# The projection of the last attention head spread over two heads, in a fused block of pooling, stick-breaking attention, delta net and MLP

## The chip, the cores and the metric

The kernel runs on one core of a Trainium2 chip, as one launch. The metric is the device time of that launch in microseconds (us). Times inside the program are counted from the start of the span of the profiled execution. The engines are TensorE (PE), VectorE (DVE), ScalarE (ACT), GpSimd (POOL) and the queue of SyncE (SP) that issues the DMAs.

## What is computed

Input x has 1024 tokens of 1024 channels, float32. Four blocks follow one another: a pooling mixer, a stick-breaking attention mixer, a gated delta net, a squared-ReLU MLP, with RMS norms between. Only the second matters here. With u the normed stream (1024 x 1024):

```
proj = u @ w_in                       # 1024 -> q 1024, k 1024, v 2048, z 2048
q, k: 16 heads of 64;  v: 16 heads of 128
z_ts = q_t . k_s / 8
A[t,s] = sigmoid(z_ts) * prod_{s<j<t} (1 - sigmoid(z_tj)),  s < t
o = A @ v
y = o * silu(z)
h = h + y @ w_out
```

## The kernel before, in words

**Numbers.** Each float32 operand of a large product is kept as a rounded part (hi) and the rest (lo), and a product is three matmuls: hi*hi, lo*hi, hi*lo. ACT rounds and DVE subtracts. For weights these are `split_weights` in both engines (L1078 and L1415), on tiles of 128 x 1024.

**The projection of a head** is three weight tiles: q and k together (64 + 64 columns), v, and the gate. Each is multiplied with all 1024 tokens in two halves of 512, each half in 8 chunks k of the contraction. `gemm_part(tile, h, k0, k1, rhs)` (L750) issues chunks k0 to k1 of half h, three matmuls for each chunk (L761 to L763), into PSUM bank 0 or 1 in turn. A projection is thus 6 halves of 8 chunks. One chunk of one half is called a unit here: 48 units, numbered in this order, 0 to 15 for q and k, 16 to 31 for v, 32 to 47 for the gate.

**A head of the attention** is NS = 12 steps. `step_of(n)` gives the piece: steps 0 to 3 and 4 to 7 are the triangular blocks of the two key halves (width 128, 256, 384, 512), steps 8 to 11 the full 512 x 512 block. Every step goes through the engines in a fixed chain:
- TensorE: `logits(n)` (L782, L783), two matmuls into banks 2 to 4
- ACT: `take_logits(n)`, sigmoid of both signs into `beta` and `stick_left`
- POOL: `mask(n)` (L536, L537) in the triangular steps
- DVE: `scan(n)` (L1523), the running product
- POOL: `weigh(n)` (L543), beta times the product, and a start value for the next scan (L548 or L553)
- TensorE: `turn_weights(n)` (L791), transposes into banks 5 and 6
- ACT: `round_weights(n)` (L1158); DVE: `rest_of_weights(n)` (L1530)
- TensorE: `values` (L804 to L806), the product with v into bank 7, once for each of three groups of four steps

**The order of work is written out by hand.** Each engine runs its own function `slots(b, first, end, ...)`, which in slot n issues the logits of step n + 3, the scan of n + 2, and the turning, rounding and rest of step n; b is the buffer of the head (0 or 1). Engines take their instructions strictly in this order and wait on semaphores. In the same slots stands the projection of the next head: TensorE issues four units a step (two ahead of and two behind `turn_weights`), DVE evacuates and scales them (`stage` into `staged` and `v_staged`, L1539; `take_gate`, L1559), `split_qk(1 - b)` splits q and k (ACT L1161 to L1163, DVE L1544 to L1548), `turn_v` (L772) transposes v through bank 7 and `split_v` (ACT L1166, DVE L1553) takes it. The gate takes its sigmoid on ACT in step 1 of its own head (L1169), two products on POOL in steps 2 and 3 (L560), and is multiplied with the output by DVE's `take_o` (L1568): half 0 in step 6, half 1 in step 1 of the next head. SP stores the output of the head to DRAM (L333).

**Loop and tail.** A loop of seven turns runs heads 0 to 13, two a turn, each with slots 2 to 11 of head b and slots 0 and 1 of the next. Written out behind it stand `slots(0, 2, NS)`, head 14 with the projection of head 15 (40 units in steps 2 to 11; units 0 to 7 are done in steps 0 and 1, in the loop), and `slots(1, 0, NS, project=False, last=True)`, the last head, without a projection. In the last head SP loads the mixed outputs of heads 0 to 7 back (`mixed_early`, L366 and L370), and ACT (L1192) and DVE (L1597) split them into the state buffers in steps 6, 7, 8, 10 and 11, as `EARLY` says. The output projection (L702 to L704) follows.

What the change touches are the four `slots` functions (POOL, TensorE, ACT, DVE), the calls of them behind the loop, and one argument in `values`.

## Time and profile before

| | us |
|---|---|
| median of 3 runs | 3315.76 |
| lowest, highest | 3312.76, 3315.87 |
| profiled execution | 3315.06 |
| its span | 3313.0 |
| TensorE busy | 3177.2 (96%) |
| DVE busy | 1723.6 (52%) |
| ACT busy | 1047.9 (32%) |
| POOL busy | 533.9 (16%) |

The span is what the profile covers, and the profiled execution's own time is 2.06 us longer. Busy time of TensorE counts overlapping matmuls once; a matmul of 512 columns is shown as lasting 0.40 us while the next one starts 0.23 us after it, so starts are to be compared, not durations. The granted clock (PEclk) is a share of full speed: 1.00 is 2.4 GHz and 0.50 is 1.2 GHz. In a row of a timeline "x4" means that four instructions are drawn together, and a bracket says how long the engine was idle before and what released it. Head 14 and the last head lie between about 1426 and 1512 us.

### The profile page before, as it was taken

The page shows a single profiled execution, that of the slowest core. Times are in us where ns is not written, and L with a number is a line of the kernel's source. Part 1 is how long each engine was busy: PE and PEld are TensorE (multiplying, and loading weights), DVE is VectorE, ACT ScalarE, POOL GpSimd, SP SyncE. Part 2 cuts the span into 40 slices and gives each one's busy share as a digit, 9 for nine tenths or more (in the row PEclk, how much of TensorE's full clock was granted, in tenths as well). Part 3 has the DMA queues.
Part 4 walks back from the last instruction along what each step waited for, and adds up shares of the span by engine and source line. Part 5 has one row for each costly group of instructions (what it writes and reads, how often), then busy time and mean ns, then how long its engine had stood idle before and what let it go on. Part 6 is the DMA issues. An engine that isn't in the chain of part 4 may idle for free.

```text
span 3313.0 us, 41664 instructions
## 1 busy us (share of the span) xinstructions
PE 3177.2 (96%) x14874; PEld 2561.5 (77%) x14874; DVE 1723.6 (52%) x1984; ACT 1047.9 (32%) x1364; POOL 533.9 (16%) x1003
## 2 busy tenths in 40 slices
PE   6999999999999999998995999999979999999998
PEld 4888888868888888877854788888767788888886
DVE  4555555647767767774233555555534423333343
ACT  3212111145545545542142444444422211111112
POOL 0000000004434434440001222222202000000001
PEclk9999999999999999999997999999969999999999
DMA  3111111121111111114103111111121111111111
GB/s 87 48 45 50 44 51 44 51 76 39 45 34 48 51 35 41 51 64 159 56 14 92 36 35 35 35 35 35 36 64 45 45 48 48 44 45 50 45 51 64
DMA packets 287554, 167.30 MB, mean 50 GB/s; under 512 B 79352, under 2 KB 273912, under 8 KB 287232
## 3 DMA queue, kind: packets, MB, share of 16 engines
q1 hardware_dynamic: 287488, 166.41, 17.3%
q8 instruction: 43, 0.70, 0.1%
q14 instruction: 23, 0.19, 0.0%
HBM read 144.33 MB, written 22.05 MB: 50 GB/s over the span
## 4 chain that ended last, share of the span: by engine, by line
PE 91%; DVE 4%; issue 1%; ACT 1%; SPq 1%; POOL 0%; DMA 0%; DVEq 0%; ACTq 0%; POOLq 0%
PE banks L702 16%; PE banks L704 16%; PE banks L703 16%; PE banks L761 8%; PE banks L762 8%; PE banks L763 8%; PE banks L791 2%; PE banks L953 1%; PE banks L894 1%; PE banks L946 1%; PE banks L711 1%; PE banks L804 1%; PE banks L806 1%; PE banks L805 1%; PE banks L783 1%
## 5 line engine op out<-in xcount | busy, mean ns | idle before, releaser
L761 PE MATMUL banks<-state_a_hi,weights_hi 128*128 128x512 f32 x1296 | 554.5, 428 | 20.9 <-DVE conv_in L1695 13.5
L762 PE MATMUL banks<-state_a_lo,weights_hi 128*128 128x512 f32 x1296 | 513.7, 396 | 0.0
L763 PE MATMUL banks<-state_a_hi,weights_lo 128*128 128x512 f32 x1296 | 513.4, 396 | 0.0
L702 PE MATMUL banks<-state_a_hi,weights_hi 128*128 128x512 f32 x1280 | 509.0, 398 | 1.9 <-DVE state_a_lo L1759 1.9
L704 PE MATMUL banks<-state_a_hi,weights_lo 128*128 128x512 f32 x1280 | 507.1, 396 | 0.0
L703 PE MATMUL banks<-state_a_lo,weights_hi 128*128 128x512 f32 x1280 | 507.0, 396 | 0.0
L1078 ACT ACTIVATE weights_hi<-weights_raw 128x1024 fp32r<-128x1024 f32 x225 | 236.7, 1052 | 646.6 <-PE banks L704 635.7
L1415 DVE TENSOR_TENSOR weights_lo<-weights_raw,weights_hi 128x1024 fp32r<-128x1024 f32 x225 | 301.1, 1338 | 137.4 <-ACT weights_hi L1078 135.1
L761 PEld LDWEIGHTS banks<-state_a_hi,weights_hi 128*128 128x128 f32 x1296 | 246.8, 190 | 62.7 <-DVE weights_lo L1415 13.9
L763 PEld LDWEIGHTS banks<-state_a_hi,weights_lo 128*128 128x128 f32 x1296 | 244.9, 189 | 58.4
L702 PEld LDWEIGHTS banks<-state_a_hi,weights_hi 128*128 128x128 f32 x1280 | 241.1, 188 | 61.0 <-DVE state_a_lo L1759 2.3
L703 PEld LDWEIGHTS banks<-state_a_lo,weights_hi 128*128 128x128 f32 x1280 | 241.1, 188 | 58.8 <-issue 0.8
L704 PEld LDWEIGHTS banks<-state_a_hi,weights_lo 128*128 128x128 f32 x1280 | 240.9, 188 | 58.3
L762 PEld LDWEIGHTS banks<-state_a_lo,weights_hi 128*128 128x128 f32 x1296 | 247.0, 191 | 37.5 <-issue 1.9
L1523 DVE TENSOR_TENSOR_SCAN stick_left<-stick_left,eps_column 128x128 f32<-128x128 f32 (+1 forms) x192 | 241.6, 1259 | 39.1 <-POOL beta L537 33.2
L702 PE MATMUL banks<-state_b_hi,weights_hi 128*128 128x512 f32 x640 | 253.5, 396 | 0.0
L704 PE MATMUL banks<-state_b_hi,weights_lo 128*128 128x512 f32 x640 | 253.1, 396 | 0.0
L703 PE MATMUL banks<-state_b_lo,weights_hi 128*128 128x512 f32 x640 | 253.1, 395 | 0.0
L543 POOL TENSOR_TENSOR beta<-beta,stick_left 128x128 f32<-128x128 f32 (+1 forms) x192 | 167.5, 872 | 424.3 <-DVE stick_left L1523 424.3
L1874 DVE TENSOR_TENSOR stream_again<-stream_again,banks 128x512 f32<-128x512 f32 (+1 forms) x80 | 54.8, 685 | 267.2 <-PE banks L704 267.2
L1530 DVE TENSOR_TENSOR weights_T_lo<-banks,weights_T_hi 128x128 fp32r<-128x128 f32 (+1 forms) x192 | 103.8, 541 | 126.7 <-ACT weights_T_hi L1158 126.7
L1158 ACT ACTIVATE weights_T_hi<-banks 128x128 fp32r<-128x128 f32 (+1 forms) x192 | 94.7, 493 | 236.7 <-PE banks L791 236.7
(265 smaller groups left out, 4788.0 us busy)
## 6 DMA issues: line engine op xcount, KB each, us to landing
weights_raw<-in_mlp_w_dram SPq DMA_DIRECT2D x64, 512.0 KB, 3.6
weights_raw<-in_gdn_w_in_dram SPq DMA_DIRECT2D x33, 512.0 KB, 4.0
weights_raw<-in_pool_w_in_dram SPq DMA_DIRECT2D x32, 512.0 KB, 3.8
weights_raw<-in_sb_w_in_dram SPq DMA_DIRECT2D x32, 512.0 KB, 4.0
weights_raw<-in_pool_w_out_dram SPq DMA_DIRECT2D x16, 512.0 KB, 3.5
weights_raw<-in_sb_w_in_dram SPq DMA_DIRECT2D x32, 256.0 KB, 4.6
mixed_dram<-stick_gate SPq DMA_DIRECT2D x16, 512.0 KB, 3.3
weights_raw<-in_sb_w_out_dram SPq DMA_DIRECT2D x16, 512.0 KB, 4.9
```

What stands on the lines that cost most here:

```text
L543: ins = pool.tensor_tensor(b, b, left[c][:, HALF - w + 1:HALF + 1], ALU.mult)
L702: pe.matmul(psum[:, bank, :], whi, hi, start=(k == 0), stop=False)
L703: pe.matmul(psum[:, bank, :], whi, lo, start=False, stop=False)
L704: last = pe.matmul(psum[:, bank, :], wlo, hi, start=False, stop=(k == kc - 1))
L761: pe.matmul(psum[:, bank, :], whi, hi, start=(k == 0), stop=False)
L762: pe.matmul(psum[:, bank, :], whi, lo, start=False, stop=False)
L763: last = pe.matmul(psum[:, bank, :], wlo, hi, start=False, stop=(k == KC - 1))
L1078: act.activation(w_hi[slot][:, :], raw[slot][:, :], ACT.Copy).then_inc(weights_hi, 1)
L1158: act.activation(aT_hi[r][:, 0:w // P, c * P:c * P + P], psum[:, 5 + n % 2, 0:w].rearrange("p (j q) -> p j q", q=P), ACT.Copy).then_inc(a_ ...
L1415: dve.tensor_tensor(w_lo[slot][:, :], raw[slot][:, :], w_hi[slot][:, :].bitcast(F32), ALU.subtract).then_inc(weights_lo, 1)
L1523: dve.tensor_tensor_scan(v, v, eps_col[:, 2:3].to_broadcast([P, w]), left[c][:, HALF:HALF + 1], ALU.mult, ALU.add).then_inc(stick_scanned, 1)
L1530: dve.tensor_tensor(aT_lo[r][:, 0:w // P, c * P:c * P + P], psum[:, 5 + n % 2, 0:w].rearrange("p (j q) -> p j q", q=P), hi, ALU.subtract). ...
```

## The change

The 40 units that steps 2 to 11 of head 14 held are spread over 16 steps, from step 2 of head 14 to step 5 of the last head: step s (counted on into the last head as 12 to 17) issues units 8 + 40(s-2)//16 to 8 + 40(s-1)//16. With them move, in the tail alone:
- DVE's staging of the second half of q and k: step 3 to 6; the split of q and k on ACT and DVE: step 4 to 7; DVE's staging of v: steps 5 and 7 to step 9 and step 0 of the last head
- the weight split of the gate tile: step 5 to 7; that of the first output tile: step 9 to step 1 of the last head
- transposes and split of v of the last head: half 0 from step 7 of head 14 to step 2 of the last, half 1 from step 3 to 4, where TensorE waits for the split of half 0 first
- in the last head the evacuation of the gate to steps 3 and 6 (it was in steps 9 and 11 of head 14), ACT's sigmoid to step 6, POOL's products to steps 7 and 8, the first `take_o` from step 6 to 9, and the second `values` from step 9 to 10
- ACT's wait for all banks, which stood ahead of the last head, to step 6 of it, ahead of the first early split

The loads on SP are unchanged. The loop is unchanged.

```diff
--- before.py
+++ after.py
@@ -270,6 +270,9 @@
             k, c = n % NS // 4, n % 4
             return k, c, HALF if k == 2 else c * P + P, (0, 1, 1)[k], (0, 1, 0)[k]
         H2 = SB_HEADS // 2 - 1
+        def last_units(s):
+
+            return range(8 + 40 * (s - 2) // 16, 8 + 40 * (s - 1) // 16) if s < 18 else ()
         N_CONST_DMA = 7
 
         x_nat = t["x"].rearrange("b (t p) d -> p (b t) d", p=P)
@@ -564,8 +567,8 @@
                         weigh(n + 2)
                     if n + 3 < NS or not last:
                         mask(n + 3)
-                    if n in (2, 3):
-                        gate(b, n - 2)
+                    if n in ((7, 8) if last else (2, 3)):
+                        gate(b, (n - 7) if last else (n - 2))
             pool.wait_ge(stream_done, 2)
             for c in range(4):
                 pool.memset(left[c][:, HALF:HALF + 1], 1.0).then_inc(ones_set, 1)
@@ -795,7 +798,7 @@
                 r = (3 * b + k) % 2
                 pe.wait_ge(a_lo_done, vl.add(4))
                 if k < 2:
-                    pe.wait_ge(v_lo_done, v_r.add(1 if turned else 0))
+                    pe.wait_ge(v_lo_done, v_r.add(int(turned)))
                 if k < 2:
                     pe.wait_ge(o_taken, ot.add())
                 for j in range(4):
@@ -805,26 +808,37 @@
                     pe.matmul(o, v_hi[b][:, token, :], aT_lo[r][:, j, c0:], start=False, stop=False, skip_group_check=True)
                     last = pe.matmul(o, v_lo[b][:, token, :], aT_hi[r][:, j, c0:], start=False, stop=(j == 3 and k != 1), skip_group_check=True)
                 last.then_inc(values_done, 1)
-            def slots(b, first, end, project=True, last=False):
+            def slots(b, first, end, ending=False, last=False):
                 for n in range(first, end):
                     if n + 3 < NS or not last:
                         logits(n + 3, b if n + 3 < NS else 1 - b)
                     if n == 1:
                         values(2, 1 - b)
-                    if n in (5, 9):
-                        values((n - 5) // 4, b, turned=n == 5 or project)
-                    if n == 0:
+                    if n in ((5, 10) if last else (5, 9)):
+                        values(n // 9, b, turned=2 * (n == 5) if last else n == 5 or not ending)
+                    if n == 0 and not ending:
                         base[0] = tile.fixed
                     piece, k0 = n // 2, 4 * (n % 2)
-                    if project:
+                    units = last_units(n + NS * last) if ending else ()
+                    def some(us):
+                        for u in us:
+                            gemm_part(base[0] + u // 16, u // 8 % 2, u % 8, u % 8 + 1, A)
+                    if not ending:
                         gemm_part(base[0] + piece // 2, piece % 2, k0, k0 + 2, A)
+                    some(units[:2])
                     turn_weights(n)
-                    if n == 3:
+                    if last and n == 2:
+                        turn_v(0)
+                    if last and n == 4:
+                        pe.wait_ge(v_lo_done, 2 * SB_HEADS - 1)
                         turn_v(1)
-                    if n == 7 and project:
+                    if n == 3 and not last:
+                        turn_v(1)
+                    if n == 7 and not ending:
                         turn_v(0)
-                    if project:
+                    if not ending:
                         gemm_part(base[0] + piece // 2, piece % 2, k0 + 2, k0 + 4, A)
+                    some(units[2:])
             norm()
             pe.wait_ge(state_lo, st_lo.add(KC))
             base = [tile.fixed]
@@ -847,8 +861,8 @@
                 for b in range(2):
                     slots(b, 2, NS)
                     slots(1 - b, 0, 2)
-            slots(0, 2, NS)
-            slots(1, 0, NS, project=False, last=True)
+            slots(0, 2, NS, ending=True)
+            slots(1, 0, NS, ending=True, last=True)
             values(2, 1)
 
             ysp = Tally()
@@ -1167,24 +1181,34 @@
             def sigmoid_gate(b):
                 act.wait_ge(sb_gate_in, gin.add())
                 act.activation(gate_sig[:, :], sb_gate[b][:, :], ACT.Sigmoid).then_inc(gate_sig_done, 1)
-            def slots(b, first, end, project=True, last=False, more=True):
+            def slots(b, first, end, ending=False, last=False):
                 for n in range(first, end):
                     if n + 3 < NS or not last:
                         take_logits(n + 3)
                     round_weights(n, b)
-                    if n == 1:
+                    if n == (6 if last else 1):
                         sigmoid_gate(b)
-                    if project:
+                    if ending and not last and n == 7:
+                        split_weights(halves.value(2))
+                        split_qk(1 - b)
+                    if last and n == 1:
+                        split_weights(halves.value(4))
+                        halves.add(6)
+                    if last and n in (2, 4):
+                        split_v(b, n // 4)
+                    if not ending:
                         if n in (1, 5, 9):
-                            (split_double if n == 9 and more else split_weights)(halves.value((n - 1) // 2))
+                            (split_double if n == 9 else split_weights)(halves.value((n - 1) // 2))
                         if n == 4:
                             split_qk(1 - b)
                         if n == 7:
                             split_v(1 - b, 0)
                         if n == NS - 1:
                             halves.add(6)
-                    if n == 3:
+                    if n == 3 and not last:
                         split_v(b, 1)
+                    if last and n == min(EARLY):
+                        act.wait_ge(bank_full, halves.value())
                     if last:
 
                         for early in EARLY.get(n, ()):
@@ -1209,9 +1233,8 @@
                 for b in range(2):
                     slots(b, 2, NS)
                     slots(1 - b, 0, 2)
-            slots(0, 2, NS, more=False)
-            act.wait_ge(bank_full, halves.value())
-            slots(1, 0, NS, project=False, last=True)
+            slots(0, 2, NS, ending=True)
+            slots(1, 0, NS, ending=True, last=True)
 
             yb = [Tally(), Tally()]
             with turns(act, 4, [(tile, 2), (landed[0], 16), (landed[1], 16), (halves, 4), (yb[0], 16), (yb[1], 16)]) as i:
@@ -1568,14 +1591,31 @@
                 dve.tensor_tensor(sb_gate[b][:, hs], sb_gate[b][:, hs], psum[:, 7, :], ALU.mult).then_inc(o_taken, 1)
                 if h == 1:
                     vd_r.add(3)
-            def slots(b, first, end, project=True, last=False):
+            def slots(b, first, end, ending=False, last=False):
                 for n in range(first, end):
-                    if n == 6:
+                    if n == (9 if last else 6):
                         take_o(b, 0)
                     if n + 2 < NS or not last:
                         scan(n + 2)
                     rest_of_weights(n, b)
-                    if project:
+                    if ending and not last:
+                        if n == 6:
+                            stage(1, staged, staged_in)
+                        if n == 7:
+                            split_weights()
+                            split_qk(1 - b)
+                        if n == 9:
+                            stage(0, v_staged, v_staged_in)
+                    if last:
+                        if n == 0:
+                            stage(1, v_staged, v_staged_in)
+                        if n == 1:
+                            split_weights()
+                        if n in (3, 6):
+                            take_gate(b, n // 6)
+                        if n in (2, 4):
+                            split_v(b, n // 4)
+                    if not ending:
                         if n in (1, 5, 9):
                             split_weights()
                         if n == 4:
@@ -1590,7 +1630,7 @@
                             take_gate(1 - b, n // 2 % 2)
                     if n == 1:
                         take_o(1 - b, 1)
-                    if n == 3:
+                    if n == 3 and not last:
                         split_v(b, 1)
                     for early in EARLY.get(n, ()) if last else ():
                         dve.wait_ge(y_split_hi, early + 1)
@@ -1622,8 +1662,8 @@
                 for b in range(2):
                     slots(b, 2, NS)
                     slots(1 - b, 0, 2)
-            slots(0, 2, NS)
-            slots(1, 0, NS, project=False, last=True)
+            slots(0, 2, NS, ending=True)
+            slots(1, 0, NS, ending=True, last=True)
             take_o(1, 1)
 
             ysh, back = Tally(KC), [Tally(), Tally()]

```

## Rows read from the trace of the kernel before

**Rows 1.** Page part 1: busy us (share of the span) and instructions of each engine

```profile
PE 3177.2 (96%) x14874; PEld 2561.5 (77%) x14874; DVE 1723.6 (52%) x1984; ACT 1047.9 (32%) x1364; POOL 533.9 (16%) x1003
```

**Rows 2.** Table of stretches (us from the span's start, engines' busy us, PEclk, DMA)

```profile
1382.90:1432.10 49.20, 49.20 (x250) 40.89 (x249) 35.71 (x40) 23.99 (x46) 20.68 (x38) 1.00 0.16 43
1432.10:1459.60 27.50, 27.50 (x141) 22.87 (x140) 24.54 (x26) 16.34 (x29) 12.76 (x20) 1.00 0.20 58
...
1472.50:1488.60 16.10, 11.87 (x59) 9.29 (x57) 10.76 (x14) 8.86 (x22) 9.49 (x20) 0.89 0.63 220
...
1488.60:1512.35 23.75, 11.75 (x47) 9.06 (x47) 20.88 (x21) 13.94 (x20) 6.74 (x10) 0.78 0.23 73
```

**Rows 3.** Waits of TensorE from 1422 to 1512: total us, times, longest

```profile
PE banks L804 <- DVE weights_T_lo L1530: 7.3, 3, 3.1
PE banks L791 <- POOL stick_left L553: 4.8, 3, 4.0
```

**Rows 4.** Timeline, TensorE: start us, us, line, operation, shape, [idle before <- releaser]

```profile
1435.79 0.40 PE L761 MATMUL banks<-state_a_hi,weights_hi 128*128 128x512 f32 x1
...
1436.95 0.40 PE L763 MATMUL banks<-state_a_hi,weights_lo 128*128 128x512 f32 x1
...
1459.58 0.22 PE L782 MATMUL banks<-k_hi_twice,q_hi_over_lo 128*128 128x128 f32 x1
...
1459.75 0.45 PE L804 MATMUL banks<-weights_T_hi,v_hi 128*128 128x512 f32 x1
...
1461.65 0.45 PE L761 MATMUL banks<-state_a_hi,weights_hi 128*128 128x512 f32 x1
...
1472.45 0.28 PE L791 MATMUL banks<-identity,beta 128*128 128x128 f32 x1
...
1483.46 0.55 PE L804 MATMUL banks<-weights_T_hi,v_hi 128*128 128x512 f32 x1 [2.77 <-DVE weights_T_lo L1530]
...
1486.79 0.55 PE L791 MATMUL banks<-identity,beta 128*128 128x128 f32 x2
...
1487.65 0.49 PE L791 MATMUL banks<-identity,beta 128*128 128x128 f32 x3
...
1508.18 0.79 PE L804 MATMUL banks<-weights_T_hi,v_hi 128*128 128x512 f32 x1 [1.41 <-DVE weights_T_lo L1530]
...
1512.35 0.40 PE L702 MATMUL banks<-state_a_hi,weights_hi 128*128 128x512 f32 x1
```

**Rows 5.** Timeline, DVE, head 14

```profile
1437.77 1.78 DVE L1523 TENSOR_TENSOR_SCAN stick_left<-stick_left,eps_column 128x256 f32<-128x256 f32 x1 [0.99 <-POOL beta L537]
...
1441.48 1.77 DVE L1523 TENSOR_TENSOR_SCAN stick_left<-stick_left,eps_column 128x384 f32<-128x384 f32 x1
...
1443.46 1.81 DVE L1544 TENSOR_TENSOR q_hi_over_lo<-projection_staged,q_hi_over_lo 64x1024 fp32r<-64x1024 f32 x1
...
1445.31 1.33 DVE L1546 TENSOR_TENSOR k_lo_twice<-projection_staged,k_hi_twice 64x1024 fp32r<-64x1024 f32 x1
...
1446.67 1.22 DVE L1548 TENSOR_TENSOR k_lo_twice<-projection_staged,k_hi_twice 64x1024 fp32r<-64x1024 f32 x1
```

**Rows 6.** Timeline, ACT: q copy of head 14, sigmoid of head 15

```profile
1441.85 1.05 ACT L1161 ACTIVATE q_hi_over_lo<-projection_staged 64x1024 fp32r<-64x1024 f32 x1
...
1476.28 1.05 ACT L1169 ACTIVATE gate_sigmoid<-stick_gate 128x1024 f32<-128x1024 f32 x1
```

**Rows 7.** Timeline, DVE, last head

```profile
1473.02 1.02 DVE L1523 TENSOR_TENSOR_SCAN stick_left<-stick_left,eps_column 128x384 f32<-128x384 f32 x1
...
1483.83 2.02 DVE L1523 TENSOR_TENSOR_SCAN stick_left<-stick_left,eps_column 128x384 f32<-128x384 f32 x1 [0.47 <-POOL beta L537]
...
1491.65 3.09 DVE L1597 TENSOR_TENSOR state_a_lo<-mixed_early,state_a_hi 128x1024 fp32r<-128x1024 f32 x2
...
1502.83 1.27 DVE L1523 TENSOR_TENSOR_SCAN stick_left<-stick_left,eps_column 128x512 f32<-128x512 f32 x1
```

**Rows 8.** Timeline, POOL: second gate product of the last head

```profile
1483.77 1.26 POOL L560 TENSOR_TENSOR stick_gate<-stick_gate,gate_sigmoid 128x512 f32<-128x512 f32 x1
```

## The prediction

> **What bounds the kernel now.** I read the busy totals first, then a table of stretches, then the waits of TensorE and the order of its instructions, last the queues of DVE, ACT and POOL around the change. TensorE is busy for 96% of the span [rows 1]: a piece of work taken off it anywhere is worth its own length, unless it waits there. The table of stretches [rows 2] shows where it does not work: a head inside the loop takes 49.2 us, all of them with TensorE busy at the full clock, while DVE has 35.7 us of work. From step 2 of head 14 (the head ahead of the last, program buffer 0) to the first logits of head 15 there are 27.5 us, again full. The last head has no projection to fill with: 11.9 of 16.1 us in its steps 0 to 5, and 11.8 of 23.8 us in steps 6 to 11, where DVE has 20.9 us of work out of 23.8 and is the bound, because the eight early splits of the mixed state stand among its scans. The granted clock is below full there (0.89 and 0.78), and the waits are those on the scan chain [rows 3]. So the change moves filler from a stretch bound by TensorE to one where it idles. At most it can give what it moves.
>
> **What is moved, in TensorE's time.** Units are k-chunks of one half of one tile, three matmuls of 512 columns. Six of them start between 1435.79 and 1436.95 at the full clock [rows 4], a pitch of 0.232 us, so a unit is 0.70 us. Head 14 had 40 of them in steps 2 to 11, four a step. Afterwards the same 40 lie over 16 steps: 8 + 40(s-2)//16 gives 25 in steps 2 to 11 of head 14 and 15 in steps 0 to 5 of head 15. Two of these 15 stand ahead of the first turning of the last head (1472.45 in [rows 4], T0 from here on). So 13 units leave the time before T0, 9.1 us, and the transposes of v half 0 go with them, 0.35 us: 9.45 us, if TensorE stays full. I do not think it does.
>
> **The wait that takes its place in head 14.** Step 9 of TensorE opens with the logits of step 0 of head 15. These need the q and k of head 15 split by DVE. Before, DVE did this in step 4, from 1443.46 to 1447.9, for a use at 1459.58: 11 us of slack [rows 4, 5]. Now its second half can only be staged at step 6, and the split stands in step 7, behind a weight split.
> DVE's time there is not set by TensorE. Its scan of step 5 waited for POOL's mask and began at 1437.77 [rows 5]; nothing that feeds it moves, so it stays. From it: the scan of step 6 from 1441.2 to 1443.0 as before (1.77), then the rest of step 4 (0.26), POOL's weighing and mask 1.9 us after the scan, and the scan of step 7 until 1446.2. Then rest of step 5, output take, scan of step 8, rest of step 6 and staging: 0.40 + 0.69 + 1.28 + 0.53 + 0.69 with some 0.1 of overlap and hand-over, 1449.9. Then scan 1.28, rest 0.66, weight split 1.23 and the three q/k instructions 1.81 + 1.33 + 1.22 = 4.36 (less overlaps of 0.08 each): about 1457.4 [rows 5]. ACT is not later: its weight rounding (1.05) and three q/k copies of 1.06 [rows 6] run from about 1450.0 to 1454.1, each ahead of the DVE instruction that needs it.
> TensorE gets to that place earlier. Up to step 9 it has 17 units instead of 28: 1459.58 - 11 x 0.70 - 0.35 = 1451.5. At step 5 it waits about 0.9 us, since the first values product needs the v split of DVE at 1440.8. So it stands at 1452.4 and waits 5.0 us for 1457.4. The logits come 2.2 us earlier than before instead of 8.1. From there to T0 it took 12.87 us; two units less (10 in place of 12) make 11.5. T0 moves from 1472.45 to 1468.9: **3.6 us gained of 9.45**. Bounds: 9.45 if DVE were in time, and 2.2 if a further wait takes the two units too.
>
> **The last head, steps 0 to 5.** Before, from T0 to the turning of step 5 (1487.65) there were 15.2 us. Of these 4.2 were waits [rows 2], and the 12 values matmuls from 1483.46 to 1486.79 took 3.3 us, where the same 12 from 1459.75 to 1461.65 took 1.9 at the full clock [rows 4]. That is 9.6 us of work. Added: 13 units and the transposes, 9.45. Added waits: the transposes of v half 0 wait for the output take of step 1, which DVE now does behind a weight split (about 0.8); the values product of step 5 waits for the chain transposes, ACT copy (0.59), DVE split (0.69) of v half 1, put one step ahead of it (about 1.2). Queued behind that product on TensorE are the last three units and the turning of step 5. Together 20 to 21 us where there were 15.2. TensorE is the bound in these steps, so DVE's additions there (staging 0.69, weight split 1.23, v split 0.69, gate 0.69) cost nothing. If TensorE had not been later they would fit in part: DVE had 10.8 of 16.1 us of work [rows 2]. The last unit ends at 1468.9 + 20.2 = 1489.1.
>
> **The last head, steps 6 to 11.** Here DVE is the bound, and three things are added.
> - The gate. DVE's second gate half (0.69) now stands in step 6, and ACT's sigmoid (1.05) waits for it, with ACT's copy of the first early chunk (1.05) behind it [rows 6]; DVE's first early split waits for that. Behind it in DVE's queue stand all later scans. Scan of step 8 about 1489.3 to 1490.6, rest 0.53, gate 0.69, then some 2.4 us of waiting, then two early splits, 2.45: 1496.6. Before, the two ended at 1494.7 [rows 7]. That is +1.9. Bounds: 0 if TensorE's part were earlier by as much, 3.1 by the sum of 0.69 and 2.4.
> - POOL's two gate products (1.28 each) move from steps 2 and 3, where TensorE is now the bound, to steps 7 and 8, beside DVE's early splits and scans. What that costs is in [rows 7, 8]: a scan of 128x384 takes 1.02 alone and 2.02 beside such a product. I take 0.9 each, +1.8; bounds 0 (if they fell into DVE's waits) and 2.0. The early splits beside a gate product are not in the trace. Beside POOL's weighing a pair took 3.09 us, where two alone take 2.45. On that the Trainium skill says ("GPSIMD Engine Reference", "Key points") that GpSimd shares its SBUF interfaces with VectorE, and that instructions with two SBUF inputs contend. The early splits are such, the gate takes from PSUM are not. By the rule nearly all of the 1.8 is paid whichever instruction is hit; by the rows of scans alone it could be 0.
> - The output take (0.69) moves from step 6, where its absence is in the times above, to step 9 ahead of the last scan, and the values product that needs it from step 9 to step 10. The last scan began at 1502.83 [rows 7]; it comes at 1502.83 + 1.9 + 1.8 + 0.65 = 1507.2. Behind the take the values product (1.9 us at the full clock, 2.9 as it ran in this stretch before) now stands ahead of the turning of steps 10 and 11, and ACT's copy of early chunk 5 ahead of its rounding of step 11. From the last scan to the last values product it took 1508.18 - 1502.83 = 5.35 us; now some 7.6 at the low clock and 6.6 at the full one.
> So the last values product begins at 1514.8 instead of 1508.18 at the low clock, +6.6. At the full clock for both products it is a good 1 + 1.4 us less, +4.2 for the first matmul of the output projection (1512.35). The clock in this stretch was between, so I take the middle: **+5.5 us**.
>
> **The sum.** Head 14 -3.6, last head about +9.1, net +5.5. Nothing after 1512.35 changes: state and weights for it are ready either way, and the DMAs that SP issues keep their order (output store and early loads hang on the output take of step 1, at 1476.9 against 1477.7). The profiled execution took 3315.06 us around a span of 3313.0; +5.5 gives 3320.6. The median of the runs, 3315.76, lies 0.7 above it, which I leave in the range. 0.2%, about what a measurement of this kernel can tell from no change, is 6.6 us; the forecast lies just inside it.
>
> **Rivals.**
> 1. The forecast, 3320.6, with 3317 to 3324 as its own range. Chance 0.50.
> 2. Faster: DVE has q and k of head 15 split by the time TensorE reaches step 9 (1452.4). This needs its chain to be 5 us shorter than by my walk, and decides from there: every us it is shorter comes off the time. Then head 14 gives 9.45 - 0.9, the last head costs the 5 us of TensorE in steps 0 to 5, and its second half shifts only: -3.5, 3311.5. With half of the second half's costs 3313 to 3314. For it: DVE has 24.5 of 27.5 us of work in that stretch before [rows 2], and less after. Against: that work does not get shorter, its place is what is late. Chance 0.20.
> 3. Slower still, by the clock. The wait of 2.77 us ahead of 1483.46, which came after little work, was followed by those 12 values matmuls in 3.3 us instead of 1.9, at or near the 1.2 GHz level [rows 4]. The new wait of 5 us in head 14 comes after full work. If the level falls there too, the next 3 to 4 us of matmuls run at 1.2 GHz, 1.5 to 2 us lost; with both values products of the second half at that level (+1.1 over my middle) it is +3: 3323.6. In the loop no wait of this kind exists, so the trace cannot tell. The Trainium skill ("TensorE: Matmul & The Clock Gate", "HAM oscillation") has it that an idle spell between groups of matmuls makes the next group start at half rate, which speaks for this rival. Chance 0.25.
> 4. The change does not do what it says: the 15 units only trade places with waits, within 1 us of before. Chance 0.05.
>
> **From these** the likeliest time is 3320.6, the range 3313.5 to 3327: it takes in most of rival 2 and all of 3. Faster by over 0.2% needs below 3309, only the end of rival 2 with no cost in the second half: 0.06. Slower by over 0.2% is above 3322.4: 0.2 of the forecast's share, most of rival 3's: 0.34. Within: 0.60.
>
> **What would show it.** Right: TensorE idle some 5 us ahead of the logits of step 0 of head 15, at about 1452, waiting for DVE's k split; the first turning of head 15 at about 1469; units among its steps 0 to 5 with short waits only; ACT's sigmoid at about 1491.5 and DVE waiting for ACT's first early copy behind it; scans or early splits of 1.8 us and more beside POOL's gate products; the last values product later than 1512. Wrong: no wait at step 9 and T0 near 1463 (rival 2), or a second half of the last head that is no longer than 23.8 us.

## The result and the profile after

| | before | after |
|---|---|---|
| median, us | 3315.61 (7 runs) | 3326.05 (7 runs) |
| lowest, highest | 3312.76, 3316.54 | 3325.08, 3327.49 |
| span of the profiled execution | 3313.0 | 3323.2 |

The changed kernel is slower: ratio 1.0034, 95% interval 1.0023 to 1.0045. That is 10.4 us by the medians and 10.2 by the spans, and it lies beyond the 0.2% of the prediction.

The engines do the same work as before, part 1 of the page [rows 1]:

```profile
PE 3177.9 (96%) x14874; PEld 2566.4 (77%) x14874; DVE 1723.2 (52%) x1984; ACT 1047.8 (32%) x1364; POOL 532.3 (16%) x1003
```

The table of stretches, cut at the same places of the program as [rows 2] (loop; step 2 of head 14 to the first logits of the last head; from there to the first turning of the last head; from there to the end of the logits of step 10, where the prediction's "steps 0 to 5" end; from there to the output projection; the third has no row there, it took 12.9 us before):

```profile
1382.90:1432.10 49.20, 49.20 (x249) 40.92 (x249) 35.74 (x40) 23.98 (x46) 20.70 (x38) 1.00 0.16 43
1432.00:1457.20 25.20, 19.81 (x103) 16.10 (x101) 20.41 (x22) 15.50 (x28) 10.97 (x20) 0.98 0.22 64
1457.20:1471.40 14.20, 14.17 (x62) 12.12 (x63) 8.35 (x10) 4.75 (x11) 4.97 (x13) 0.80 0.00 0
1471.40:1492.90 21.50, 19.66 (x104) 16.06 (x103) 12.60 (x18) 9.14 (x21) 8.27 (x20) 1.00 0.50 171
1492.90:1522.20 29.30, 11.60 (x46) 9.25 (x45) 20.96 (x20) 14.75 (x21) 8.64 (x10) 0.65 0.17 54
```

The loop is unchanged. The second row is 25.2 us where it was 27.5, but holds 5.4 us of idle TensorE. The third is longer than the 12.9 us before, although it has two units less: the granted clock is 0.80. The fourth, which took in the 13 units, is 5.4 us longer (16.1 before), and the last 5.55 us (23.75 before) with no unit added to it; the clock is 0.65 in it (0.78 before). The waits of TensorE from 1422 on (us in total, times, longest), which answer to [rows 3]:

```profile
PE banks L794 <- POOL stick_left L556: 7.6, 2, 6.8
PE banks L807 <- DVE stick_gate L1591: 7.1, 1, 7.1
PE banks L785 <- DVE k_lo_twice L1571: 4.6, 1, 4.6
PE banks L807 <- DVE weights_T_lo L1553: 3.9, 2, 3.1
```

Two of them are new in kind: the wait for the k split (L785, 4.6) and the one for DVE's output take (L807 for L1591, 7.1). The timeline of TensorE at the first of them, which answers to [rows 4]:

```profile
1452.08 0.60 PE L794 MATMUL banks<-identity,beta 128*128 128x128 f32 x4
1457.23 0.48 PE L785 MATMUL banks<-k_hi_twice,q_hi_over_lo 128*128 128x128 f32 x1 [4.55 <-DVE k_lo_twice L1571]
...
1457.72 0.74 PE L807 MATMUL banks<-weights_T_hi,v_hi 128*128 128x512 f32 x1
1458.25 0.63 PE L808 MATMUL banks<-weights_T_lo,v_hi 128*128 128x512 f32 x1
...
1462.62 0.52 PE L764 MATMUL banks<-state_a_hi,weights_hi 128*128 128x512 f32 x1
...
1471.40 0.27 PE L794 MATMUL banks<-identity,beta 128*128 128x128 f32 x1
```

The logits come at 1457.23 after 4.55 us of waiting. Behind them the matmuls of 512 columns start 0.43 to 0.53 us apart, the 1.2 GHz level, until about 1462.6. So the first turning of the last head comes at 1471.40, 1.05 us earlier than before, for 9.45 us of work taken out ahead of it. The second half of the last head:

```profile
1491.47 0.40 PE L785 MATMUL banks<-k_hi_twice,q_hi_over_lo 128*128 128x512 f32 x1
...
1510.20 0.76 PE L807 MATMUL banks<-weights_T_hi,v_hi 128*128 128x512 f32 x1 [7.06 <-DVE stick_gate L1591]
...
1513.74 1.22 PE L794 MATMUL banks<-identity,beta 128*128 128x128 f32 x8
1518.02 0.80 PE L807 MATMUL banks<-weights_T_hi,v_hi 128*128 128x512 f32 x1 [3.05 <-DVE weights_T_lo L1553]
...
1522.22 0.40 PE L705 MATMUL banks<-state_a_hi,weights_hi 128*128 128x512 f32 x1
```

DVE, the q/k split and the second half, against [rows 5, 7]:

```profile
1453.45 1.22 DVE L1567 TENSOR_TENSOR q_hi_over_lo<-projection_staged,q_hi_over_lo 64x1024 fp32r<-64x1024 f32 x1
1454.70 1.22 DVE L1569 TENSOR_TENSOR k_lo_twice<-projection_staged,k_hi_twice 64x1024 fp32r<-64x1024 f32 x1
1455.95 1.22 DVE L1571 TENSOR_TENSOR k_lo_twice<-projection_staged,k_hi_twice 64x1024 fp32r<-64x1024 f32 x1
...
1496.91 2.36 DVE L1637 TENSOR_TENSOR state_a_lo<-mixed_early,state_a_hi 128x1024 fp32r<-128x1024 f32 x2 [2.12 <-ACT state_a_hi L1216]
...
1502.71 2.29 DVE L1546 TENSOR_TENSOR_SCAN stick_left<-stick_left,eps_column 128x512 f32<-128x512 f32 x1
...
1505.51 3.95 DVE L1637 TENSOR_TENSOR state_a_lo<-mixed_early,state_a_hi 128x1024 fp32r<-128x1024 f32 x2
...
1509.97 1.27 DVE L1546 TENSOR_TENSOR_SCAN stick_left<-stick_left,eps_column 128x512 f32<-128x512 f32 x1
```

ACT's sigmoid of the last gate, and the first early copies behind it, and POOL's two gate products, against [rows 6, 8]:

```profile
1494.88 1.06 ACT L1183 ACTIVATE gate_sigmoid<-stick_gate 128x1024 f32<-128x1024 f32 x1 [1.28 <-DVEq L1585]
1495.84 1.99 ACT L1216 ACTIVATE state_a_hi<-mixed_early 128x1024 fp32r<-128x1024 f32 x2
```

```profile
1501.98 1.94 POOL L563 TENSOR_TENSOR stick_gate<-stick_gate,gate_sigmoid 128x512 f32<-128x512 f32 x1
...
1506.38 1.99 POOL L563 TENSOR_TENSOR stick_gate<-stick_gate,gate_sigmoid 128x512 f32<-128x512 f32 x1
```

DVE waits 2.12 us for the first early copy (1496.91). Its scan of step 10 beside POOL's first gate product took 2.29 us, and the pair of early splits beside the second 3.95. POOL's products took 1.94 and 1.99 us, where the one in [rows 8] took 1.26.

### The profile page after: what moved, and what is told of

It is laid out like the page before. It is cut to its first block, busy times and chain, and to the rows that moved or that the text cites. A ratio compares the mean times of both kernels' runs of the same rounds, so it can differ in the third digit from the quotient of the medians.

```text
span 3323.2 us, 41664 instructions
## 1 busy us (share of the span) xinstructions
PE 3177.9 (96%) x14874; PEld 2566.4 (77%) x14874; DVE 1723.2 (52%) x1984; ACT 1047.8 (32%) x1364; POOL 532.3 (16%) x1003
## 4 chain that ended last, share of the span: by engine, by line
PE 91%; DVE 3%; ACT 1%; issue 1%; SPq 1%; POOL 1%; DMA 0%; DVEq 0%; ACTq 0%; POOLq 0%
PE banks L705 16%; PE banks L707 16%; PE banks L706 16%; PE banks L764 8%; PE banks L765 8%; PE banks L766 8%; PE banks L794 2%; PE banks L908 1%; PE banks L967 1%; PE banks L960 1%; PE banks L807 1%; PE banks L809 1%; PE banks L808 1%; PE banks L786 1%; PE banks L714 1%
```

## The experiments

All edits are in the tail only. Whole runs of this kernel scatter by some microseconds between jobs, so I compare places in the trace, one trace for each kernel. One distance runs from the first turning of head 14 (1424.56 before) to the first turning of the last head ("head 14"), one from there to the first matmul of the output projection ("last head"). The unchanged head 14 gave 47.89, 47.90 and 47.89 us in three traces. Where a wait is followed by a low clock the distance varies more: 46.90, 46.58, 46.62 and 47.17 in the four with head 14 as changed.

The last head ends with a values product of 12 matmuls of 512 columns, and this took between 2.9 and 5.3 us, as the clock was high or low in it. So the column "to last values" gives the distance from the first turning of the last head to the start of this product. It was 46.62, 46.92 and 46.63 us in after, e1 and e2, whose last heads are alike but for one unit less in e2.

| kernel | head 14 | last head | of it, to last values | sum | sum against before | whole kernel, ratio (95% interval) |
|---|---|---|---|---|---|---|
| before | 47.89 | 39.90 | 35.73 | 87.79 | | |
| after | 46.90 | 50.82 | 46.62 | 97.72 | +9.93 | 1.0034 (1.0023 to 1.0045) |
| e1_busy_wait | 44.32 | 51.15 | 46.92 | 95.47 | +7.68 | 1.0048 (1.0031 to 1.0065) |
| e2_qk_early | 42.79 | 50.91 | 46.63 | 93.70 | +5.91 | 1.0023 (1.0011 to 1.0034) |
| e6_fill_before | 45.48 | 49.34 | 45.16 | 94.82 | +7.03 | 1.0021 (1.0011 to 1.0031) |
| e3_tail_only | 47.90 | 43.40 | 39.14 | 91.30 | +3.51 | 1.0009 (0.9999 to 1.0019) |
| e3b_take_only | 47.89 | 44.02 | 38.74 | 91.91 | +4.12 | 1.0012 (1.0002 to 1.0021) |
| e7_turn_first | 46.58 | 47.27 | 44.38 | 93.85 | +6.06 | 1.0022 (1.0013 to 1.0032) |
| e9_sigmoid_behind | 46.62 | 49.40 | 44.95 | 96.02 | +8.23 | 1.0017 (1.0007 to 1.0026) |
| e11_narrow_gate | 47.17 | 50.00 | 44.88 | 97.17 | +9.38 | 1.0017 (1.0006 to 1.0027) |
| e10_three_mended | 41.22 | 48.00 | 42.71 | 89.22 | +1.43 | 1.0005 (0.9996 to 1.0015) |
| e5_half_gate | 44.53 | 39.47 | 34.96 | 84.00 | -3.79 | 0.9992 (0.9983 to 1.0001) |

### The wait in head 14

**e1_busy_wait**, from the changed kernel:

```diff
 # TensorE, slots
+if ending and not last and n == 9:
+    pe.wait_ge(o_taken, ot.value(1))
+    for _ in range(18):
+        pe.matmul(psum[:, 7, :], w_hi[(base[0] + 1) % 2][:, 0:P], A_hi[:, 0, 0:HALF], start=True, stop=True, ...)
 if n + 3 < NS or not last:
     logits(n + 3, b if n + 3 < NS else 1 - b)
```

> The changed kernel with 18 extra matmuls of 512 columns into the free bank 7, ahead of the logits of step 0 of the last head, where TensorE waited 4.55 us for the k split (they are thrown away). Theory (the wait itself costs the clock): these take 4.2 us of the wait, the granted clock stays at 1.00 behind it, the values product and the two units after it run at a pitch of 0.23 us instead of 0.43, the first turning of the last head comes 2.5 us earlier (1471.4 to 1468.9), and the kernel takes about 3323.5. Rival (the level falls there for another reason, as the load of the other engines): the pitch is 0.43 again, the turning stays at 1471.4, the kernel at 3326.

Timeline of TensorE in this kernel:

```profile
1451.66 4.44 PE L816 MATMUL banks<-state_a_hi,weights_hi 128*128 128x512 f32 x18
1456.46 0.33 PE L785 MATMUL banks<-k_hi_twice,q_hi_over_lo 128*128 128x128 f32 x1 [0.36 <-DVE k_lo_twice L1575]
...
1456.73 0.45 PE L807 MATMUL banks<-weights_T_hi,v_hi 128*128 128x512 f32 x1
1457.02 0.39 PE L808 MATMUL banks<-weights_T_lo,v_hi 128*128 128x512 f32 x1
...
1468.04 0.27 PE L794 MATMUL banks<-identity,beta 128*128 128x128 f32 x1
```

The 18 matmuls fill 4.44 us, the logits keep their place, and the values product behind them starts at a pitch of 0.23 us instead of 0.43 to 0.53. By the table head 14 is 2.58 us shorter than after. This shows that the wait costs twice: what it lasts, and the clock behind it. The values product behind it took 1.91 us here and 3.52 in each of the four traces that have this wait unfilled (after, e7, e9, e11). The whole kernel did not show the gain: 3326.87 us by the median of 4 runs from 3320.9 to 3332.9, the widest scatter here.

**e2_qk_early**, from the changed kernel:

```diff
+# last_units: units 4s to 4s+3 for s = 2, 3; then 16 + 32(s-4)//14 to 16 + 32(s-3)//14
 # ACT
-n == 7: split_weights(halves.value(2)); split_qk(1 - b)
+n == 4: split_qk(1 - b)
+n == 7: split_weights(halves.value(2))
 # DVE
-n == 6: stage(1, staged, staged_in);  n == 7: split_weights(); split_qk(1 - b)
+n == 3: stage(1, staged, staged_in);  n == 4: split_qk(1 - b);  n == 7: split_weights()
```

> The changed kernel with units 8 to 15 (second half of q and k) back at four a step in steps 2 and 3, their staging and the split of q and k back in steps 3 and 4, and the other 32 units spread over steps 4 to 17. All of the placement in the last head stays. Theory (the late q/k split takes what head 14 should give): no wait ahead of the logits of step 0 of the last head, the clock stays full, the first turning of the last head comes at about 1464.6, 6.8 us earlier than in the changed kernel, its steps 0 to 5 hold one unit less (0.7), and the kernel takes about 3318.6: still no gain over before, since the second half of the last head keeps its 9 us. Rival (DVE, packed in steps 4 to 9, holds TensorE back anyway): the turning at 1469 or later, 3323.5 or more.

The wait for the k split is gone, and head 14 is 4.1 us shorter than after, where 6.8 was expected. TensorE now waits for POOL at the turning of step 7, a wait that neither kernel had (timeline of TensorE; the last two rows show the pitch behind the wait):

```profile
1450.64 0.66 PE L796 MATMUL banks<-identity,beta 128*128 128x128 f32 x4 [1.89 <-POOL stick_left L553]
...
1452.25 0.63 PE L787 MATMUL banks<-k_hi_twice,q_hi_over_lo 128*128 128x512 f32 x1
1452.68 0.63 PE L788 MATMUL banks<-k_lo_twice,q_hi_over_lo 128*128 128x512 f32 x1
```

DVE's scan of step 7 stands behind the three q/k instructions (they end at 1447.03, the scan starts at 1447.07), POOL's weighing behind the scan, and TensorE gets there earlier than it can be served. Behind this wait of 1.89 us nine matmuls start up to 0.43 us apart (1451.06 to 1454.79), which costs about 1.6 us against a pitch of 0.23 (in e10 below, with the same code here, the clock did not fall). So both theories had a part: the late split cost most, and with the split early the filler in head 14 was needed to cover the scan chain. The last head stayed at 50.9 us.

**e6_fill_before**, from the changed kernel:

```diff
-range(8 + 40 * (s - 2) // 16, 8 + 40 * (s - 1) // 16)
+range(8 + 23 * (s - 2) // 7, 8 + 23 * (s - 1) // 7)  if s < 9
+range(31 + 17 * (s - 9) // 9, 31 + 17 * (s - 8) // 9)
 # DVE: stage(0, v_staged) in step 8 instead of 9
```

> The changed kernel with the 40 units in another spread: 23 of them in steps 2 to 8 (17 before) and 17 in steps 9 to 17, and the staging of v half 0 one step earlier; the q/k split stays in step 7. Theory: the logits of step 0 of the last head stay at 1457.3, as DVE sets them, but the wait shrinks from 4.55 us to about 0.4 (six units of 0.7 in it), the clock stays full, three units less stand between them and the first turning, which comes at about 1466.7, and three less behind it: the kernel at about 3319.2. Rival (TensorE is held elsewhere, by banks not yet free or by the scans): new waits of the same 4 us in steps 7 to 11, turning at 1471, 3326.

Timeline of TensorE, the longer of its two waits in this stretch (the other is 0.59 us at 1451.60, for DVE's staging):

```profile
1460.36 0.33 PE L787 MATMUL banks<-k_hi_twice,q_hi_over_lo 128*128 128x128 f32 x1 [2.27 <-DVE k_lo_twice L1573]
```

The logits did not keep their place: 34.45 us behind the first turning of head 14 instead of 32.73. More units ahead of step 7 make TensorE's turning of that step later, ACT rounds it before it copies q and k, and so the split moves with the filler. The wait fell only to 2.27, and 1.4 us came off head 14 where 4.7 were expected. The clock fell behind this shorter wait too: the values product that follows took 2.90 us, where it took 1.91 in e1. The expectation took DVE's time as fixed; that held for the change and not for a denser spread.

### The last head

**e3_tail_only**, from the kernel before:

```diff
 # POOL:    gate products in steps 7, 8 of the last head (2, 3)
 # TensorE: values(1) in step 10 of the last head (9)
 # ACT:     sigmoid_gate in step 6 of the last head (1)
 # DVE:     take_o(b, 0) in step 9 of the last head (6)
```

> The kernel before, with nothing of the projection moved, and only the placement in the last head changed as in the change: sigmoid in step 6, POOL's gate products in steps 7 and 8, the output take in step 9 and the second values product in step 10. Theory (DVE-bound second half: sigmoid ahead of the first early copy 1.0, two gate products beside splits and scans 2.0, the values product ahead of two turnings 2.2, less up to 2 for the scans of steps 3 and 4 that no longer stand beside the products): the first matmul of the output projection at 1515.5 to 1517.8 instead of 1512.35, the kernel 3 to 5.5 us slower than before. Rival (the second half grows only because the projection reaches into the last head): within 1 us of before.

The last head is 3.5 us longer with no unit moved into it, inside the expected range. Timeline of DVE, scans of steps 5, 6 and 10:

```profile
1482.05 0.75 DVE L1523 TENSOR_TENSOR_SCAN stick_left<-stick_left,eps_column 128x256 f32<-128x256 f32 x1 [0.99 <-POOL beta L537]
...
1484.47 1.02 DVE L1523 TENSOR_TENSOR_SCAN stick_left<-stick_left,eps_column 128x384 f32<-128x384 f32 x1 [0.48 <-POOL beta L537]
...
1497.82 2.28 DVE L1523 TENSOR_TENSOR_SCAN stick_left<-stick_left,eps_column 128x512 f32<-128x512 f32 x1
```

The scans of steps 5 and 6, beside which POOL no longer multiplies, fall from 1.75 to 0.75 and from 2.02 to 1.02 [rows 7 for the latter], and the one of step 10 rises to 2.28. The shorter scans come first and the longer ones later, so in this kernel the two effects work against each other. In the changed kernel I take it that only the second counts, since TensorE is the bound in steps 0 to 5; no run separates this.

**e3b_take_only**: of these four edits only those of TensorE and DVE.

> The kernel before with only the first output take of the last head moved to step 9 and the second values product to step 10; sigmoid and POOL products stay. With the run that moved all four (3.5 us by the length of the last head) it divides that cost. Theory: the values product ahead of the two turnings costs 1.6 to 2.2 us (last head 41.5 to 42.1 us instead of 39.9), the sigmoid and POOL's products the other 1.3 to 1.9. Rival (POOL's products beside splits and scans are the whole): under 0.5 us here.

4.12 us, twice what was expected and more than with all four. TensorE waits 5.1 us for the output take ahead of the turning of step 10. Timeline of TensorE, start of the last values product and what follows it:

```profile
1510.78 0.80 PE L804 MATMUL banks<-weights_T_hi,v_hi 128*128 128x512 f32 x1 [3.06 <-DVE weights_T_lo L1530]
...
1516.06 0.63 PE L702 MATMUL banks<-state_a_hi,weights_hi 128*128 128x512 f32 x1
```

Up to the last values product this pair of edits costs 3.01 us and all four cost 3.41, so moving the sigmoid and the gate products adds only 0.4 here, net of the two shorter scans. That the whole last head is longer than with all four is the clock: the last values product took 5.28 us, all at the 1.2 GHz level, where it took 4.26 in e3.

**e7_turn_first**, from the changed kernel:

```diff
-values(1) ahead of turn_weights(10) in the last head
+turn_weights(10); values(1)
```

> The changed kernel with TensorE's turning of step 10 of the last head ahead of the second values product instead of behind it. Theory (the take at step 9 holds the turnings of steps 10 and 11 in TensorE's queue): the turning of step 10 at about 1506.5 instead of 1513.9, the last values product 2.2 us earlier (after the first turning of the last head by 44.4 us instead of 46.6), the kernel at about 3323.9. Rival (the end hangs on the scan of step 11 and DVE's early splits only): no change.

Timeline of TensorE:

```profile
1505.60 1.12 PE L794 MATMUL banks<-identity,beta 128*128 128x128 f32 x4 [3.35 <-POOL stick_left L556]
1509.32 0.77 PE L807 MATMUL banks<-weights_T_hi,v_hi 128*128 128x512 f32 x1 [2.60 <-DVE stick_gate L1593]
...
1514.87 0.50 PE L807 MATMUL banks<-weights_T_hi,v_hi 128*128 128x512 f32 x1 [1.41 <-DVE weights_T_lo L1555]
...
1517.76 0.50 PE L705 MATMUL banks<-state_a_hi,weights_hi 128*128 128x512 f32 x1
```

The turning of step 10 starts at 1505.60 instead of 1513.74, and the last head is 3.55 us shorter. Of this the order gives the expected 2.2 (46.62 to 44.38 up to the last values product). The other 1.3 us are the clock: this product takes 2.9 us (1514.87 to 1517.76) where it took 4.2 in the changed kernel (1518.02 to 1522.22). They can't be credited to the order: e10 below has the same order and the same 1.41 us of waiting ahead of the product, and there it took 5.29 us.

**e9_sigmoid_behind**, from the changed kernel:

```diff
 # ACT, step 6 of the last head
-sigmoid_gate(b); early copies 0, 1
+early copies 0, 1; sigmoid_gate(b)
```

> The changed kernel with ACT's sigmoid of the last gate behind the first two early copies in step 6 instead of ahead of them. Theory (DVE waits 2.12 us for the copy, 1.05 of it for the sigmoid ahead of it): the wait is 1.05 us shorter and the first output matmul 1.05 us earlier (49.8 us after the first turning of the last head instead of 50.8). Rival (the copy waits for the last unit of TensorE or for the early loads, not for the sigmoid): no change.

DVE's waits for ACT's early copies fall from 2.4 us in two waits to one of 0.3:

```profile
DVE state_a_lo L1639 <- ACT state_a_hi L1216: 0.3, 1, 0.3
```

The wait for the first copy is gone whole, since the copy no longer waits for the gate's evacuation either. Up to the last values product the last head is 1.67 us shorter, more than the 1.05 expected, and 1.42 as a whole.

**e11_narrow_gate**, from the changed kernel:

```diff
-hs = slice(h * HALF, h * HALF + HALF)
+hs = slice(h * HALF, h * HALF + (8 if narrow else HALF))   # narrow in the last head
```

> The changed kernel with POOL's two gate products of the last head over 8 columns instead of 512 (part of the gate is left out). Theory (they contend with DVE's scans and early splits: the scan of step 10 took 2.29 us where 1.27 is usual, the pair of early splits 3.95 where 2.95 was): both return to 1.3 and 2.95 us, and the last head is 2.0 us shorter (48.8 us from its first turning to the first output matmul instead of 50.8). Rival (DVE's longer times come from something else, such as ACT's copies at the same time): no change.

Timeline of DVE (scan of step 10, early splits of step 8, scan of step 11), then of POOL:

```profile
1505.13 1.27 DVE L1546 TENSOR_TENSOR_SCAN stick_left<-stick_left,eps_column 128x512 f32<-128x512 f32 x1
...
1506.90 2.89 DVE L1637 TENSOR_TENSOR state_a_lo<-mixed_early,state_a_hi 128x1024 fp32r<-128x1024 f32 x2
...
1510.31 1.27 DVE L1546 TENSOR_TENSOR_SCAN stick_left<-stick_left,eps_column 128x512 f32<-128x512 f32 x1
```

```profile
1504.40 0.87 POOL L563 TENSOR_TENSOR stick_gate<-stick_gate,gate_sigmoid 128x8 f32<-128x8 f32 x1
...
1507.78 0.93 POOL L563 TENSOR_TENSOR stick_gate<-stick_gate,gate_sigmoid 128x8 f32<-128x8 f32 x1
```

The scan takes 1.27 us instead of 2.29 and the pair 2.89 instead of 3.95, as expected. The last scan starts 8.6 us after the end of the first early pair instead of 10.7, so the contention cost 2.1 us there, and 1.74 up to the last values product. But the last head as a whole is only 0.8 us shorter: the last values product took 5.12 us, all of it at the 1.2 GHz level, instead of 4.20.

**e10_three_mended**: e2, e7 and e9 in one kernel.

> The changed kernel with three of its losses mended at once: q and k early (as in e2), the turning of step 10 ahead of the second values product (as in e7), the sigmoid behind the first early copies (as in e9). Distances are from the first turning of head 14 to the first output matmul: 87.8 us before, 97.7 in the changed kernel, 93.7 with e2 alone; e7 took 3.55 off the last head, e9 1.42. Theory (separate losses that add up): 88.7 us, 1 us longer than before, so the spread by itself brings nothing even then. Rival (they overlap; the second half is set by DVE's work): 91 us or more.

89.22 us, against 88.7 expected, but the sum agrees in part by luck. Timeline of TensorE, the wait of e2 in head 14 and the last values product:

```profile
1452.18 0.66 PE L796 MATMUL banks<-identity,beta 128*128 128x128 f32 x4 [1.89 <-POOL stick_left L553]
...
1509.17 0.79 PE L809 MATMUL banks<-weights_T_hi,v_hi 128*128 128x512 f32 x1 [1.41 <-DVE weights_T_lo L1560]
```

Up to the last values product the last head is 3.91 us shorter than after, and e7 and e9 alone gave 2.24 and 1.67: these two losses do add up. Head 14 has the code of e2 and the same wait of 1.89 us, but here the granted clock stayed at 1.00 behind it, and head 14 is 1.57 us shorter than in e2. The last values product ran at the 1.2 GHz level throughout and took 5.29 us, for 4.28 in e2. If both chances are left out, by taking the distance up to the last values product with the full clock in head 14, 41.22 + 42.71 us stand against 47.89 + 35.73 before: 0.31 us more. So the spread as a whole brings nothing even with the three losses mended.

**e5_half_gate**, from the kernel before, moves what fits into the idle time:

```diff
+# last_units: 4 a step in steps 2 to 5; 24 + 16(s-6)//6 ... in 6 to 11; 40 + 2(s-12), two a step, in 0 to 3 of the last head
 # DVE: stage(1, v_staged) in step 8 (7); take_gate(0) in step 11 (9); take_gate(1) in step 4 of the last head (11 of head 14)
-sigmoid_gate(b) on 1024 columns in step 1
+sigmoid on 512 columns in steps 1 and 5 of the last head
-POOL's products in steps 2, 3
+POOL's products in steps 2, 10
 # ACT's wait for all banks in step 6 of the last head instead of ahead of it
```

> The kernel before, with only the second gate half moved: units 8 to 23 in steps 2 to 5 as before, 24 to 39 over steps 6 to 11, and 40 to 47 two a step in steps 0 to 3 of the last head, where TensorE waited 4.2 us. The q/k split, the v split and the first output take stay where they were; the gate's evacuation, sigmoid and POOL product go half by half, the second half in steps 4, 5 and 10 of the last head. Theory (the loss is in what was made late, not in filling the last head): the first turning of the last head comes 5.6 us earlier than before by its distance from the first turning of head 14 (42.3 instead of 47.9), the last head lasts 40 to 41.5 us to the first output matmul (39.9 before), so the kernel gains 4 to 5 us. Rival (a last head with a projection in it always gives back what head 14 gains, as its scan chain sets the pace): the same within 1 us.

Stretches of its last head, cut as in [rows 2] but for the inner cut, which stands 0.5 us later:

```profile
1469.90:1485.40 15.50, 14.29 (x77) 11.32 (x75) 9.95 (x14) 8.42 (x22) 8.27 (x19) 1.00 0.53 189
1485.40:1509.40 24.00, 13.00 (x47) 9.98 (x48) 20.77 (x21) 13.70 (x19) 8.69 (x11) 0.64 0.30 97
```

The last head holds six more units and is 0.4 us shorter than before: TensorE is busy for 14.3 of 15.5 us in its first half, at the full clock, and the values product of step 5 has lost the slow clock of [rows 4]. The sum is 3.8 us less than before, just under the 4 to 5 expected. I had put the first turning 2.2 us too early (42.3 for 44.53). Of this 1.4 is that two of the eight units stand ahead of it, so 4.2 us leave head 14 and not 5.6; TensorE idles for 0.45 us in head 14, and the rest I have not traced. The medians are 3311.3 (11 runs) against 3313.74 (33 runs), but the interval of the ratio, 0.9983 to 1.0001, includes no change. It is the only kernel here whose ratio is below 1, and it beats the changed kernel clearly (1.0034, 1.0023 to 1.0045); a gain over the kernel before is seen only between the marks of one trace.

## Why the prediction was right or wrong

The time lay in the range of 3313.5 to 3327, 1 us below its upper end. The way was right, the size was not: the likeliest forecast was +5.5 us, and +9.9 were measured between the two places in the trace. Of the 4.4 us between forecast and measurement, 2.6 are in head 14 (1.0 gained for 3.6) and 1.8 in the last head (10.9 lost for 9.1). I gave 0.34 to slower by over 0.2% and 0.60 to no change; the first came true.

**Units and what leaves head 14: right.** The pitch stayed 0.23 us where the clock was full.

**The wait for the q/k split: right.** The logits were put at 1457.4 after 5.0 us and came at 1457.23 after 4.55. The walk's intermediate points hold too, such as the values product of step 5 (0.87 us of waiting for 0.9). In part it is luck that the end came out: the split was faster than its rows of before, 3 x 1.22 instead of 4.36, for POOL was idle beside it from 1452.6 on, and the weight split ahead of it slower, 1.83 instead of 1.23, and the two offset each other.

**From these logits to the first turning: the failed step.** I took 11.5 us, "two units less make 11.5", and it took 14.2. The 2.7 us are the clock but for 0.1, and I had the clock as rival 3 and not in the forecast. e1 shows it: with the wait filled, the same stretch takes 11.6 us. Rival 3's price of 1.5 to 2 us was low too, as the level stayed low for 5 us of matmuls.

**Steps 0 to 5 of the last head: right.** 20 to 21 us were given where there were 15.2. The 1487.65 that I had called the turning of step 5 is that of step 6 (three transposes, x3); the same place comes at 1491.93 after the change, 20.5 us behind the first turning. The two waits are 0.83 and 1.0 for 0.8 and 1.2. The last unit ends at the logits of step 9, 1491.47, 2.4 us later than given, and that is the 2.5 us of the step before.

**Steps 6 to 11: the mechanisms were right, the sum a little small.** The wait for the first early copy was 2.12 us (2.4 given), each gate product cost 1.0 (0.9 given), and the last scan came 38.6 us after the first turning (38.3 given). From the last scan to the last values product it took 8.05 us, for 7.6 at the low clock. I had then taken the middle of the two clock levels; both values products ran at the low one, the first whole and the second for its first half. The last head grew by 10.9 us instead of 9.1. Counted up to the last values product, e7 takes off 2.24 us, e9 1.67 and e11 1.74, which confirms the order of the values product, the sigmoid and the gate products as causes. Together they are 5.65 us, and from the logits of step 9 to that product the last head had grown by 5.46; e7 and e9 were also run together and add up, e11 was run only alone.

**The rule on the shared SBUF interfaces** (the Trainium skill, "GPSIMD Engine Reference", "Key points") agrees with the trace: the early splits, with two SBUF inputs, took 3.95 us for two beside a gate product and 2.89 beside a narrow one. **The rule of rival 3** (the Trainium skill, "TensorE: Matmul & The Clock Gate", "HAM oscillation") is what the trace shows here: an idle spell of 4.55 us ended in the 1.2 GHz level, and where it was filled the matmuls behind it kept a pitch of 0.23 us.

**Rivals.** Rival 2 fell: DVE was late by what was said. e2, which takes that lateness away, shows that even then head 14 gives 5.1 us and not 8.6, and 6.7 in e10, where the clock did not fall; 0.7 of what is missing is one unit more in head 14. Rival 4 fell. Rival 3 held in head 14 and in the second half; its 3323.6 was the nearest.

What stays open: when the clock falls behind the shorter waits. Behind the same wait of 1.89 us it fell in e2 and not in e10. Behind the same wait of 1.41 us the last values product took 4.17 us before, 2.89 in e7 and 5.29 in e10. With one trace for each kernel I can't tell an effect of the edit from chance here, so up to 2.4 us of a last head's length may not be the edit's.

## What to carry to other kernels

Before filler is moved into an idle stretch, find the engine that bounds that stretch, and count what has to move with the filler: here 9.45 us of TensorE's work were moved, head 14 became 1.0 us shorter, and the last head 10.9 longer: about 5.4 where TensorE took the units in, and 5.5 in the second half, where the gate, the output take and the values product landed in queues on the bounding path. Give an idle stretch only what fits its idle time and whose consumers are not urgent (eight units, the second half of the gate), and leave early what another engine needs long to prepare. A new wait on TensorE can cost twice, its length and the slow matmuls behind it, as it did in the changed kernel. And compare variants up to a mark ahead of the stretch whose clock varies.

## What the runs showed of the hardware

- After full work, 4.55 us of waiting on TensorE were followed by 5 us of matmuls at the 1.2 GHz level, 2.6 us lost (e1 against the changed kernel). This was so in all four traces with that wait. A wait of 1.89 us in the same head was followed by a granted clock of 0.59 over 4.2 us in e2 and of 1.00 in e10, with the same code there. Matmuls whose result is thrown away kept the level up for no cost in head 14.
- The same 12 matmuls of 512 columns, behind the same wait of 1.41 us, took 2.89 us in e7, 4.17 before and 5.29 in e10.
- Contention of POOL and DVE is paid by both sides with the early splits (POOL's product 1.94 to 1.99 us instead of 1.26 to 1.29, a pair of splits 3.95 instead of 2.89). A product of 8 columns still took 0.87 and 0.93 us beside them, though it delayed DVE no longer; a weighing of 128 columns took 0.41 us (POOL, 1436.41 before). No run shows the narrow product by itself.
